# A DiT block on one core: the up projection's units multiplied channel group by channel group

## What is computed

```python
D_MODEL = 2048
SEQ = 256
D_FF = 5632

def conv_ffn(h, w_up, conv_w, conv_b, w_down):
    u = h @ w_up
    ch = u.shape[-1]
    u = lax.conv_general_dilated(
        u, conv_w[:, None, :].astype(u.dtype), window_strides=(1,),
        padding=((CONV_WIDTH // 2, CONV_WIDTH // 2),),
        dimension_numbers=('NWC', 'WIO', 'NWC'), feature_group_count=ch) + conv_b
    gate, up = jnp.split(u, 2, axis=-1)
    return (jax.nn.silu(gate) * up) @ w_down
```

## Time and profile before

| | |
|---|---|
| median of 3 runs | 1714.55 us (1714.19 to 1715.43) |
| the profiled execution, its own time | 1711.75 us |
| its span, first to last instruction | 1710.1 us |
| PE busy | 1669.2 us, 98% of the span |
| DVE busy | 1089.2 us, 64% |
| ACT busy | 757.4 us, 44% |
| mean granted TensorE clock | 0.996 of full speed |

### The profile page before, as it was taken

The page is one execution under the profiler, slowest core; times in us unless marked ns, Lnnn a source line. Parts: engine busy times, 40 slices in busy tenths (PEclk is TensorE's granted clock), DMA queues, the critical chain, the costliest instruction groups (busy, mean ns, idle before and its releaser), DMA issues.

```text
span 1710.1 us, 23893 instructions
## 1 busy us (share of the span) xinstructions
PE 1669.2 (98%) x8832; PEld 1372.2 (80%) x8832; DVE 1089.2 (64%) x1372; ACT 757.4 (44%) x971; POOL 108.4 (6%) x161
## 2 busy tenths in 40 slices
PE   5999999999999999999999999999999999999997
PEld 2568888788888678888888788888888888888886
DVE  3338788768896775554555766666666666655556
ACT  4333322623222664444444555555555555544444
POOL 0003232122121000000000000000000000000000
PEclk8999999999999999999999999999999999999999
DMA  9999897279895137566665566666666665666652
GB/s 352 386 370 365 309 337 259 77 254 320 264 311 181 51 117 261 189 189 192 190 239 192 145 205 187 189 191 186 192 186 189 190 185 185 199 193 194 194 192 82
DMA packets 161814, 371.48 MB, mean 217 GB/s; under 512 B 11671, under 2 KB 12423, under 8 KB 160598
## 3 DMA queue, kind: packets, MB, share of 16 engines
q1 hardware_dynamic: 140240, 291.65, 53.0%
q0 software_dynamic: 20144, 74.22, 12.7%
q10 hardware_dynamic: 1366, 4.74, 0.7%
HBM read 368.36 MB, written 2.21 MB: 217 GB/s over the span
## 4 chain that ended last, share of the span: by engine, by line
PE 95%; DMA 2%; DVE 2%; issue 1%; ACT 0%; SPq 0%; DVEq 0%; POOL 0%; ACTq 0%
PE ps L2011 20%; PE ps L2010 10%; PE ps L2025 10%; PE ps L2027 10%; PE ps L2026 10%; PE ps L2380 5%; PE ps L2379 5%; PE ps L2378 5%; PE ps L1915 4%; PE ps L1916 3%; PE ps L1917 3%; DMA raw<-in_ada_w 2%; PE ps L1907 2%; PE ps L2008 1%; PE ps L2094 1%; PE ps L2076 1%
## 5 line engine op out<-in xcount | busy, mean ns | idle before, releaser
L1218 DVE TENSOR_TENSOR w_lo<-raw,w_hi 128x1024 fp32r<-128x1024 f32 x475 | 578.6, 1223 | 411.0 <-ACT w_hi L719 410.5
L719 ACT CAST w_hi<-raw 128x1024 fp32r<-128x1024 f32 x475 | 498.3, 1050 | 759.7 <-PE ps L2027 273.2
L2011 PE MATMUL ps<-h2T,w_hi 128*128 128x512 f32 x1320 | 462.4, 394 | 0.0
L2010 PE MATMUL ps<-h2T,w_lo 128*128 128x256 f32 x1320 | 366.5, 278 | 0.0
L2011 PEld LDWEIGHTS ps<-h2T,w_hi 128*128 128x128 f32 x1320 | 247.5, 188 | 53.7
L2010 PEld LDWEIGHTS ps<-h2T,w_lo 128*128 128x128 f32 x1320 | 247.9, 188 | 3.9
L2025 PE MATMUL ps<-w_hi,hT 128*128 128x512 f32 x512 | 201.6, 394 | 0.0
L1294 DVE SCALAR_TENSOR_TENSOR ada_acc<-ada_raw,silu_c,ada_acc 128x512 f32<-128x512 f32 x240 | 180.1, 750 | 30.6 <-DMA ada_raw<-in_ada_w 14.8
L2027 PE MATMUL ps<-w_hi,hT 128*128 128x512 f32 x512 | 199.4, 389 | 0.0
L2026 PE MATMUL ps<-w_lo,hT 128*128 128x512 f32 x512 | 199.3, 389 | 0.0
L642 POOL DMA_DIRECT2D ada_raw<-in_ada_w x128 | 91.0, 712 | 376.5 <-DVE ada_acc L1294 217.8
(11 more groups left out here) (240 smaller groups left out, 2059.4 us busy)
## 6 DMA issues: line engine op xcount, KB each, us to landing
raw<-in_ffn_w_up SPq DMA_DIRECT2D x176, 512.0 KB, 3.8
raw<-in_w_in SPq DMA_DIRECT2D x147, 512.0 KB, 4.7
ada_raw<-in_ada_w POOLq DMA_DIRECT2D x128, 512.0 KB, 6.1
raw<-in_ffn_w_down SPq DMA_DIRECT2D x88, 512.0 KB, 4.3
raw<-in_ada_w SPq DMA_DIRECT2D x64, 512.0 KB, 9.7
raw<-in_w_out SPq DMA_DIRECT2D x32, 512.0 KB, 3.9
raw<-in_w_branch_a SPq DMA_DIRECT2D x16, 512.0 KB, 3.7
raw<-in_w_branch_b SPq DMA_DIRECT2D x16, 512.0 KB, 3.7
```

What stands on the lines that cost most here:

```text
L719: act.copy(w_hi[:, s % SPLIT_SLOTS, :], raw[:, s, :]).then_inc(hi_ready[s], 1)
L1218: dve.tensor_tensor(w_lo[:, s % SPLIT_SLOTS, :], raw[:, s, :], w_hi[:, s % SPLIT_SLOTS, :], ALU.subtract).then_inc(lo_ready[s], 1)
L2010: pe.matmul(ps[:, b + t, 0:SEQ], w_lo[:, row4(s), at], high(kc), start=False, stop=False)
L2011: return pe.matmul(o, w_hi[:, row4(s), at], both(kc), start=False, stop=(kc == KC - 1))
```

## The change

It turns round the two loops of every unit of the up projection that ran tile by tile. Before: for each of four tiles, both channel groups. After: for the first channel group all four tiles, and then for the second group all four. The matmuls, their operands, the order of sums within a bank and the wait and signal at the ends of the unit stay; the unit of job 0 that already had this order is not touched.

```diff
@@ -2354,8 +2354,9 @@
                     else:
                         if ready:
                             pe.wait_ge(h2T_ready, s + 2)
-                        for t in range(TILES):
-                            mm = unit_paired(s, t, b, both, high)
+                        for i in range(2):
+                            for t in range(TILES):
+                                mm = products_paired(s, t, b, i, both, high)
                     mm.then_inc(used[s], 1)
                     if ready and s + 4 < KC // 2:
                         pe.wait_ge(modulated2_ready, 2 * s + 2)
```

## The result

The changed kernel takes 1723.62 us (median of 5 runs, 1721.40 to 1723.93), the kernel before 1714.19 us (5 runs, 1711.78 to 1715.43). The ratio is 1.0054, with a 95% interval of 1.0043 to 1.0065: slower by 7 to 11 us. The forecast, 1714.5 us with a range up to 1719.4, was wrong.

What follows compares the result with a forecast made beforehand. The prediction took PE's matmul time to bound the kernel. Its terms summed 0 + 0 + 0 + 0, leaving 1711.75 us in the profiled execution and 1714.5 us on the runs' scale, range 1711.0 to 1719.4.

Steps and rivals of the forecast that it cites:

- What bounds the kernel: Up projection: PE's matmul time bounds it, no idle time there, weights ready 5.75 us ahead, 0.3469 us a pair.
- Waits, nothing: Up projection units: slots and banks are waited for and released at the same matmul counts, so no wait is added.
- More changes of bank: 175 changed units: eight bank changes each in place of four, 700 more, priced zero, -2.1 to +2.1 us.
- The same activations four times running: Changed units: the moving operand changes every fourth pair instead of each pair; priced at zero.
- that rival: Every changed unit: the new order costs 0.025 us each, +4.4 us, 1718.9 us; chance 0.03.
- The first unit of a job: 21 first units: seven meetings of equal widths lost, one kept; priced zero, at most 0.05 us each, 1.0 us.
- slow rhythm: Pace read from job 1 on PE: 22.59 us a job against 22.20 in the loop, 0.39 us more without waits.
- The rival: Jobs 2 to 21 on PE take job 1's slower pace: +7.8 us, 1722.4; chance 0.08 for all, 0.05 for half.
- The clock: Up projection: PE's granted clock falls to 1.2 GHz, over 300 us more, above 2000 us; chance 0.01.

Runs made afterwards that it cites:

- E2: Changed kernel with the first unit of each job put back to the old order, units two to eight group by group: 1713.55 us, ratio 0.9997 to the kernel before.
- E10: Changed kernel, but every unit goes group by group within two tiles at a time: 1712.16 us (one run).
- E1: Changed kernel with only the first unit of each job group by group, the others tile by tile: 1722.81 us, ratio 1.0053 to the kernel before.
- E9: Changed kernel, but in the second half of a job's first unit pairs run narrow, wide, then wide, narrow in turn: 1717.55 us (one run).
- E4: Changed kernel put back to tile by tile, with every pair of a job's first unit run wide, narrow: 1717.21 us (one run).
- E3: Changed kernel with the first pair of each job's fifth unit turned to wide, narrow: 1716.10 us (one run).
- E5: Changed kernel with one pair turned to wide, narrow in each of the third, fifth and seventh units of every job: 1717.58 us (one run).
- E6: Changed kernel put back to tile by tile, with every unit's pairs run wide, narrow, narrow, wide: 1715.86 us (one run).
- E8: Changed kernel with jobs 2 and 3 written out straight and nine loop turns in place of ten: 1723.44 us (one run).

## Why the prediction was wrong, point by point

- **What bounds the kernel: right.** PE alone, with no idle time in the up projection in either kernel. The weights of the fourth unit of job 10 were ready 5.75 us ahead before and some 5.9 us ahead after (subtraction done at 1203.88, unit begun at 1201.31 + 3 x 2.83 = 1209.8).
- **Waits, nothing: right.** No wait of PE appeared.
- **More changes of bank, zero within 2.1 us either way: right.** E2 and E10 have them and keep 22.20 and 22.21 us.
- **The same activations four times running, zero: right.** E2 has that as well. The 0.02 us of the earlier trace rows were no price by unit, and that rival falls with them: E2's jobs are not longer.
- **The first unit of a job: the step that failed.** I priced its new order inside the unit, at zero, with 0.05 us in 21 units as the upper end. (Of the seven meetings of equal widths inside the unit one is kept, so it loses six, not seven; the price did not use the number.) In its own unit the order does cost next to nothing (2.81 us against 2.79). But it hands the following seven units to the slow rhythm: the 20 looped jobs take 452.13 in place of 443.99 us, +8.1 us (0.41 a job), less 0.4 in job 1, +7.7 us. The interval of the ratio, 7 to 11 us, holds that. The medians differ by 9.4 us; the 1.7 us beyond the 7.7 are placed by no run, and in the profiles all that is left of the difference lies ahead of job 1, where executions of one kernel differ too.
- **The rival was right in place and size.** "Jobs 2 to 21 on PE", 0.39 us a job, +7.8 us, 1722.4: the runs show 1723.62. What was wrong is its chance of 0.08, and a range that stopped short of it. (The range adds 0.5 us of scatter at its upper end and 1 us at its lower, which is not the same amount twice as it says; either would have fallen short.) Its size was read from job 1 and holds, and its ground, that the first unit lost the meetings of equal widths, is what E1 and E9 bear out. That all of the loop went slow and not every second job, as in E4 and E9, nothing in the prediction could tell. I let "20 jobs out of 20 in the loop run fast" count as evidence against it. They are no twenty cases: the looped jobs run the same instructions, and from job 3 on each is entered at the same point of the same pattern, so they are one case or two, and the trace had three or four in all. Job 1 (slow behind the old order) and job 0 (fast behind the new one) said that either order can end in either rhythm. That should have made the slow loop something like one chance in three, by my estimate.
- **The clock: no part in the change.** The Trainium skill's rule on cycling through banks ("TensorE: Matmul & The Clock Gate", psum-queue depth-cycling) did not show here: E10 changes bank at every pair, its looped jobs take 22.21 us where those of before take 22.20, and the granted clock is 1.00 throughout its loop, as in the changed kernel's.

## What to carry to other kernels

When PE is never idle and a mere change of order is to be costed, read the start-to-start steps, not the waits, and look whether the same stream of matmuls runs at two paces somewhere in the trace. If it does, take either pace as possible behind an edit that changes which widths follow each other, and count all turns of a loop together as one case. A result of this size says little about the idea behind the edit: here group by group is as good as tile by tile, provided that the job's first unit is left alone.

## What the hardware showed that I had not expected

- A stream of alternating 512- and 256-column matmuls, each with its own 128-column weight load, runs at 0.347 us a pair or at 0.353 us a pair, and keeps its pace through the 56 pairs of seven units. The slow pace is marked by a longest wide duration of 403 ns, the fast one by 395 or 396 (391 in its other form).
- In these runs it changes pace only where equal widths meet (a job's start, wide behind wide, is such a place as well): one turned pair, which makes two such meetings, does it (E3, E5), in either direction. Where they meet all the time (E6) there is a third, fixed pace, 22.29 us a job.
- Which pace follows is decided by the order of widths and by where in its pattern of two or three pairs the stream stands at the meeting: the table behind E8 has no exception. The inherited pace alone does not decide (out of the 392 and 395 form an alternating start goes slow, out of the 391 form it stays fast). What stays open is why: no run here looks inside a pair.
- The granted clock in the first unit of the up projection was full in 3 profiles of 12 and had fallen in the other 9, which costs 0.9 to 2.0 us of a run and shows no tie to the kernels' edits, which all lie behind it.
